# Routing the last token tile from values ahead of its layer norm, in a two-layer hybrid encoder step

## The reference, cut to what matters

```python
x = layernorm(DN_ALPHA * x + merged @ lp['w_out'], lp['ln1_g'], lp['ln1_b'])
moe_out = hier_moe(x, ...)
ple_term = jax.nn.sigmoid(x @ lp['w_ple_gate']) * (ple @ lp['w_ple'])
x = layernorm(DN_ALPHA * x + moe_out + ple_term, lp['ln2_g'], lp['ln2_b'])

def layernorm(x, g, b):            # mu, var over the row
    return (xf - mu) * lax.rsqrt(var + EPS) * g + b

# hier_moe: group logits x @ w_rg (4), expert logits x @ w_re (4 groups x 8)
g_top, g_idx = lax.top_k(softmax(x @ w_rg), 1)
e_top, e_idx = lax.top_k(softmax(e_logits of group g_idx), 2)
# each token goes to its two experts; h = silu(xb @ w1) * (xb @ w3); h @ w2; weighted sum
```

## Time and profile before

| | |
|---|---|
| time, median of 3 (lowest, highest) | 1543.61 us (1542.16, 1543.89) |
| profiled execution, its span | 1542.58 us, 1540.7 us |
| PE busy, weight loads | 1287.2 us (84%), 714.5 us (46%) |
| DVE, ACT, POOL busy | 400.0 (26%), 264.9 (17%), 56.3 us (4%) |
| memory traffic | 490.87 MB, mean 319 GB/s |
| mean granted clock | 0.928 |
| chain that ended last, by engine | PE 56%, DMA 33%, SP's queue 6%, DVE 3% |

### The profile page before, as it was taken

One profiled execution on the slowest core, in us unless ns is written; L12 is line 12 of the kernel. 1 busy time (PEld: TensorE's weight loads), 2 busy tenths in 40 slices (PEclk: granted clock), 3 DMA queues, 4 the chain that ended last, 5 costly groups with the idle time before them and its releaser, 6 DMA issues.

```text
span 1540.7 us, 20136 instructions
## 1 busy us (share of the span) xinstructions
PE 1287.2 (84%) x8464; PEld 714.5 (46%) x8465; DVE 400.0 (26%) x1021; ACT 264.9 (17%) x692; POOL 56.3 (4%) x98
## 2 busy tenths in 40 slices
PE   7999999999976766756699999999998766767655
PEld 4766887544431322322276678766353322313311
DVE  4142633532101101101133446245221101011003
ACT  2342422020100000000044434212110000000001
POOL 1300000000000000000022010000000000000000
PEclk9999999999988978888899999999999979879868
DMA  9503435989999999999972043578999999999994
GB/s 330 162 1 110 171 117 179 416 338 426 426 427 426 427 427 427 426 427 426 409 235 83 19 151 112 178 259 351 414 427 426 426 427 426 427 427 425 427 425 180
DMA packets 100047, 490.87 MB, mean 319 GB/s; under 512 B 9552, under 2 KB 15600, under 8 KB 52464
## 3 DMA queue, kind: packets, MB, share of 16 engines
q1 hardware_dynamic: 94912, 476.46, 75.8%
q0 software_dynamic: 5040, 13.03, 2.8%
HBM read 486.56 MB, written 2.89 MB: 318 GB/s over the span
## 4 chain that ended last, share of the span: by engine, by line
PE 56%; DMA 33%; SPq 6%; DVE 3%; issue 1%; ACT 0%; POOL 0%; DVEq 0%
PE bank L971 55%; DMA arena<-in_w_e_gate 12%; DMA arena<-in_w_e_up 9%; SPq L768 4%; DMA ring<-in_w_e_down 4%; DMA ring<-in_w_e_up 4%; SPq L834 2%; DMA ring<-in_w_e_gate 2%; DMA arena<-in_w_e_down 2%; PE bank L1021 2%; DMA ring<-in_w_in 1%; DVE arena L2062 0%; DVE arena L1950 0%; DVE x_sb L1959 0%; ACT xT L1570 0%
## 5 line engine op out<-in xcount | busy, mean ns | idle before, releaser
L971 PE MATMUL bank<-arena 128*32 128x512 f32 (+12 forms) x2696 | 496.9, 542 | 122.4 <-DMA arena<-in_w_e_gate 34.3
L971 PE MATMUL bank<-ring,arena 128*32 128x512 f32 (+4 forms) x1376 | 345.1, 645 | 2.7 <-ACT arena L1899 2.7
L971 PEld LDWEIGHTS bank<-arena 128*32 128x32 f32 (+4 forms) x2696 | 186.5, 138 | 335.6 <-issue 322.1
L971 PE MATMUL bank<-ring,xT 128*32 128x128 f32 (+5 forms) x1536 | 238.0, 364 | 1.4 <-ACT xT L1570 1.1
L971 PE MATMUL bank<-xT,ring 128*128 128x288 f32 x768 | 191.8, 407 | 0.0
L971 PEld LDWEIGHTS bank<-ring,xT 128*32 128x32 f32 (+1 forms) x1536 | 121.9, 137 | 101.1 <-issue 90.9
L971 PEld LDWEIGHTS bank<-xT,ring 128*128 128x128 f32 x768 | 143.7, 190 | 37.9
L971 PE MATMUL bank<-cst,arena 128*32 128x512 f32 x144 | 90.2, 785 | 57.2 <-DMA arena<-in_w_e_up 24.8
L971 PEld LDWEIGHTS bank<-ring,arena 128*32 128x32 f32 (+1 forms) x1376 | 87.4, 129 | 45.8 <-issue 36.6
L971 PE MATMUL bank<-arena,x_sb 128*128 128x128 f32 (+1 forms) x768 | 99.7, 282 | 1.4 <-DVE arena L2282 0.8
L971 PEld LDWEIGHTS bank<-arena,x_sb 128*128 128x128 f32 (+1 forms) x768 | 90.5, 190 | 20.1 <-issue 13.3
(11 more groups left out here) (225 smaller groups left out, 845.7 us busy)
## 6 DMA issues: line engine op xcount, KB each, us to landing
arena<-in_w_e_gate SPq DMA_DIRECT2D x68, 1024.0 KB, 26.0
arena<-in_w_e_up SPq DMA_DIRECT2D x62, 1024.0 KB, 26.5
arena<-in_w_e_down SPq DMA_DIRECT2D x58, 1024.0 KB, 26.3
ring<-in_w_e_up SPq DMA_DIRECT2D x48, 1024.0 KB, 26.6
ring<-in_w_e_gate SPq DMA_DIRECT2D x44, 1024.0 KB, 26.5
ring<-in_w_e_down SPq DMA_DIRECT2D x42, 1024.0 KB, 26.9
ring<-in_w_in SPq DMA_DIRECT2D x32, 1024.0 KB, 9.4
lb<-in_w_e_gate SPq DMA_DIRECT2D x14, 1024.0 KB, 25.9
```

Of the source, the lines that this page charges most:

```text
L971: return pe.matmul(out, lhsT, rhs, start=first, stop=last, skip_group_check=True)
```

## The change

Tile 1 is routed from its mixed values, ahead of the layer norm. With m the mean and r the inverse deviation of a row, the logits are

    ((x - m) * r * g + b) @ wr  =  r * (x @ (g * wr)  -  m * (g @ wr))  +  b @ wr

- POOL loads g and b of the first norm as columns (`norm_cols`, 16 numbers per partition) from a new input laid out on the host (`ln1_cols`). DVE multiplies the router's weights by g (`wr_scaled`).
- PE transposes the mixed tile (`turn_raw`), each half when DVE has written it (`x_mixed`), around `half_mix(1, 1)`. ACT copies both halves into xT.
- `router_sums` makes g @ wr and b @ wr, one row of 72 numbers, ACT moves it out of PSUM with the first half negated, `spread_sums` spreads it over 128 partitions, ACT moves it again.
- `router(1)` takes the raw transposes and `wr_scaled`; DVE corrects the logits in two operations, and the 14 routing operations follow.
- The norm's first pass runs ahead of the routing on DVE. The second pass (`shift_half`) runs in halves: one between the routing and `place_tile(1)`, one behind it. `ln_out` of tile 1 is signalled then.
- The transposes of the normalized tile (`turn_mixed(1)`), needed by its ple products, move behind "G" of quad 0, and PE waits for their copies ahead of `plain(0, 1)`.

```diff
@@ -214,7 +214,7 @@
             (("rt", 2), 7), (("t1", 0, 0), 0), (("t1", 0, 1), 1), (("wo", 0, 1), 6), (("rt", 0), 3),
-            (("rk", 2), 4), (("rk", 0), 5), (("wo", 1, 1), 2), (("t1", 1, 0), 0), (("t1", 1, 1), 1), (("rt", 1), 3),
+            (("rk", 2), 4), (("rk", 0), 5), (("raw", 0), 0), (("wo", 1, 1), 2), (("sw",), 7), (("raw", 1), 1), (("sb",), 7), (("rt", 1), 3),
             (("pl", 0, 2), 2), (("pg", 0, 2), 5), (("rk", 1), 4), (("XT0", 0), 6), (("XT0", 1), 7), (("cnt",), 3)]
@@ -237,7 +237,8 @@
     combine = [(job, b) for job, b in zip(COMBINE_JOBS, (7, 0, 1, 2, 3))]
-    j = [(("G",), 0)] + plain(0, 1, 2, 3) + ([(("ST0",), 4)] if g == 0 else []) + [(("U",), 1)] + plain(1, 0, 7, 0)
+    turned = [(("t1", 1, 0), 5), (("t1", 1, 1), 6)] if g == 0 else []
+    j = [(("G",), 0)] + turned + plain(0, 1, 2, 3) + ([(("ST0",), 4)] if g == 0 else []) + [(("U",), 1)] + plain(1, 0, 7, 0)
     if g:
...
@@ -531,6 +532,11 @@
         acc_s = carve(4544, D)
+        norm_cols = carve(0, 2, 8)
+        wr_scaled = carve(16, 8, 36)
+        wr_sums = carve(304, 72)
+        wr_sums_all = carve(376, 72)
+        raw_logits = carve(448, 36)
         scaled_s = carve(3072, 2 * P)
...
@@ -940,6 +949,7 @@
                 pool.dma_start(pT[:, :, SEQ:T], p_sample[layer]).then_inc(ple_in, 16)
+                pool.dma_start(norm_cols, ln1_cols[layer].rearrange("p (k c) -> p k c", k=2)).then_inc(norm_cols_in, 16)
                 job_read(pool, (layer, "bra", 3))
@@ -1289,17 +1299,34 @@
                         if c % 4 == 0:
-                            job_read(pe, (layer, "t1", t, c // 4))
-                        ins = mm(b[0:NT[t], 0:36], xT[:, c, T0[t]:T0[t] + NT[t]], wr[:, c, :], c == 0, c == 7)
+                            job_read(pe, (layer, "raw", c // 4) if t == 1 else (layer, "t1", t, c // 4))
+                        ins = mm(b[0:NT[t], 0:36], xT[:, c, now(t)], (wr_scaled if t == 1 else wr)[:, c, :], c == 0, c == 7)
                     done(ins)
+                def turn_raw(h):
+
+                    pe.wait_ge(x_mixed, 2 * layer + h + 1)
+                    transposes(layer, ("raw", h), [((c % 4) * P, P, x[0:P, 1, c * P:c * P + P]) for c in range(4 * h, 4 * h + 4)])
+
+                def router_sums():
+
+                    pe.wait_ge(norm_cols_in, 16 * (layer + 1))
+                    b = open_bank((layer, "sw"))
+                    for k in range(2):
+                        for c in range(8):
+                            ins = mm(b[0:1, 36 * k:36 * k + 36], norm_cols[:, k, c:c + 1], wr[:, c, :], k + c == 0, c == 7)
+                    done(ins)
+
+                def spread_sums():
+
+                    job_read(pe, (layer, "sw"))
+                    b = open_bank((layer, "sb"))
+                    done(mm(b[:, 0:72], ones[0:1, :], wr_sums[0:1, :], True, True))
+
                 def turn_mixed(t):
                     for h in range(2):
-                        if t == 1 and h == 0:
-                            pe.wait_ge(x_half, 2 * layer + 2)
-                        else:
-                            pe.wait_ge(ln_out, ln_place(2 * layer + 1, t))
+                        pe.wait_ge(ln_out, ln_place(2 * layer + 1, t))
                         transposes(layer, ("t1", t, h), [((c % 4) * P, P, x[0:NT[t], t, c * P:c * P + P]) for c in range(4 * h, 4 * h + 4)])
                 def plain_low(j, t):
@@ -1342,6 +1369,10 @@
                         for t in tiles:
+                            if t == 1 and h == 0:
+                                pe.wait_ge(x_half, 2 * layer + 2)
+                            elif t == 1:
+                                pe.wait_ge(ln_out, ln_place(2 * layer + 1, t))
                             for c in range(4):
@@ -1359,11 +1390,15 @@
                 rank(0)
+                turn_raw(0)
                 half_mix(1, 1)
+                router_sums()
+                turn_raw(1)
+                spread_sums()
+                pe.wait_ge(wr_scaled_out, layer + 1)
+                router(1)
                 pe.wait_ge(sel_early, layer + 1)
                 gather_first((2, 0))
-                turn_mixed(1)
-                router(1)
                 pe.wait_ge(ple_in, 32 * (layer + 1))
@@ -1489,6 +1524,9 @@
                     if g == 0:
+                        turn_mixed(1)
+                        for h in range(2):
+                            job_read(pe, (layer, "t1", 1, h))
                         plain(0, 1)
@@ -1834,9 +1872,25 @@
-                for t in MIX_ORDER:
+                def read_raw(h):
+
+                    key = (layer, "raw", h)
+                    job_done(act, key)
+                    emptied(act.copy(xT[:, 4 * h:4 * h + 4, now(1)], transposed(bank(key), 1)), key)
+
+                for t in (2, 0):
                     layer_norm(1 + 2 * layer, (t,))
-                    read_x("t1", layer, t, (0, 1) if t != 1 else (0,))
+                    read_x("t1", layer, t, (0, 1))
+                read_raw(0)
+                key = (layer, "sw")
+                job_done(act, key)
+                act.activation(wr_sums[0:1, 0:36], bank(key)[0:1, 0:36], ACT.Copy, scale=-1.0)
+                emptied(act.copy(wr_sums[0:1, 36:72], bank(key)[0:1, 36:72]), key)
+                read_raw(1)
+                layer_norm(1 + 2 * layer, (1,))
+                key = (layer, "sb")
+                job_done(act, key)
+                emptied(act.copy(wr_sums_all, bank(key)[:, 0:72]), key)
                 for t in MIX_ORDER:
@@ -1889,6 +1943,7 @@
                     if g == 0:
+                        read_x("t1", layer, 1, (0,))
                         plain_gate(0, 1)
@@ -2244,6 +2299,8 @@
                     job_read(dve, key)
+                    if t == 1:
+                        dve.sem_inc(x_mixed, 1)
                     step(half_stats(t, x[:, t, :], j))
@@ -2256,15 +2313,26 @@
                     job_done(dve, key)
+                    if t == 1:
+                        job_read(dve, (layer, "sb"))
+                        dve.wait_ge(ln_rstd, ln_place(1 + 2 * layer, t))
+                        step(dve.scalar_tensor_tensor(raw_logits, wr_sums_all[:, 0:36], mvs[:, 2:3], b[:, 0:36], ALU.mult, ALU.add))
+                        step(dve.scalar_tensor_tensor(raw_logits, raw_logits, ln_rs[:, 1:2], wr_sums_all[:, 36:72], ALU.mult, ALU.add))
+                        dve.sem_inc(bank_emptied[book.bank(key)], 1)
+                        b = raw_logits
                     step(dve.tensor_copy(lg[:, 0:4], b[0:n, 0:4]))
                     step(dve.max(r[:, 0:8], lg[:, 0:8]))
                     step(dve.max_index(ri[:, 8:16], r[:, 0:8], lg[:, 0:8]))
                     step(dve.tensor_copy(r[:, 16:17], ri[:, 8:9]))
                     step(dve.tensor_scalar(r[:, 48:52], iota[0:n, 0:4], r[:, 16:17], 2 * BIG, ALU.is_equal, ALU.mult))
-                    emptied(dve.scalar_tensor_tensor(lg[:, 8:40].rearrange("p (g e) -> p g e", g=GROUPS), bcast(r[:, 48:52], 2, PER_GROUP),
-                                                     BIG, b[0:n, 4:36].rearrange("p (g e) -> p g e", g=GROUPS),
-                                                     ALU.subtract, ALU.min), key)
-                    job_read(dve, key)
+                    ins = dve.scalar_tensor_tensor(lg[:, 8:40].rearrange("p (g e) -> p g e", g=GROUPS), bcast(r[:, 48:52], 2, PER_GROUP),
+                                                   BIG, b[0:n, 4:36].rearrange("p (g e) -> p g e", g=GROUPS),
+                                                   ALU.subtract, ALU.min)
+                    if t == 1:
+                        step(ins)
+                    else:
+                        emptied(ins, key)
+                        job_read(dve, key)
                     step(dve.max(r[:, 24:32], lg[:, 8:40]))
@@ -2289,6 +2357,8 @@
+                dve.wait_ge(norm_cols_in, 16 * (layer + 1))
+                dve.tensor_tensor(wr_scaled, wr, bcast(norm_cols[:, 0, :], 2, 36), ALU.mult).then_inc(wr_scaled_out, 1)
                 for t in (2, 0):
@@ -2303,10 +2373,24 @@
                 mixed(1, 1)
-                normalize(1 + 2 * layer, 1, x[:, 1, :], x_half)
-                read_x("t1", layer, xT, (1,))
+                at = ln_place(1 + 2 * layer, 1)
+                dve.bn_aggr(mvs[:, 2:4], ln_st).then_inc(ln_var, 1)
+                dve.wait_ge(ln_var, at)
+                job_done(dve, (layer, "raw", 1))
+                for h in range(2):
+                    half = x[:, 1, 512 * h:512 * h + 512]
+                    ins = dve.scalar_tensor_tensor(half, half, mvs[:, 2:3], lnw[:, 0, 512 * h:512 * h + 512], ALU.subtract, ALU.mult)
+                step(ins)
                 route_tile(1)
+
+                def shift_half(h):
+
+                    half = x[:, 1, 512 * h:512 * h + 512]
+                    return dve.scalar_tensor_tensor(half, half, ln_rs[:, 1:2], lnw[:, 1, 512 * h:512 * h + 512], ALU.mult, ALU.add)
+
+                shift_half(0).then_inc(x_half, 1)
```

(3 more changed lines are left out.)

8 lines of the change are left out of this document (6 added, 2 removed).

## The result

The changed kernel takes 1552.41 us (median of 8 runs, 1549.63 to 1558.61), the kernel before in the same runs 1543.46 (1542.01 to 1548.1). The ratio is 1.0056, 95% interval 1.0045 to 1.0067: slower by about 0.56%, by the medians 8.95 us, outside the range given. The profiled execution took 1552.71, its span is 1550.9, the mean granted clock 0.932.

The account below looks back on a forecast made before the run. The expert weight stream bounds the kernel, PE's work the start of G. Per layer +1.2 on G less 0.4 for the seam gives +0.8, for two layers +1.6: 1543.61 + 1.6 = 1545.2 us, range 1542.6 to 1548.8.

Parts of the forecast that it names:

- What bounds the stretch: Routing ahead of G of quad 0: PE's own work, almost without gaps, sets G's start, not the small vector operations.
- Rival A: Routing: the vector chain decides, so G begins 2.3 us a layer earlier and the time is 1538.9; chance 0.06.
- only change places: PE ahead of `rank(1)`: router product (1.88 us), gathers (4.25) and ple products (2.4) are reordered, adding nothing to the sum.
- The sum at full clock: PE's products put ahead of `rank(1)` less those taken off: G starts 1.2 us later per layer, ends +0.2 and +2.6.
- (a): PE ahead of `rank(1)`: the four transposes of `turn_raw(0)` add 0.5 us.
- (b): PE ahead of `rank(1)`: the 16 products of `router_sums` (32 rows in fp32) add 1.4 us, from 0.7 to 2.2.
- rival C: `router_sums` costs the count row's rate and the hand-off is long: +5.2 us in all, 1548.8; chance 0.13.
- (c): PE ahead of `rank(1)`: `turn_raw(1)` within the wait for ACT's reads, then `spread_sums`: 1.05 us, range 0.7 to 1.6.
- the 1.75 taken off: PE ahead of `rank(1)`: tile 1's transposes with their wait (1.37 us) and the rank product's wait (0.38) go.
- The seam: SP's queue: the later norm-slot piece lets the half pieces find a running stream, gaining 0.4 us a layer, between 0 and 0.9.
- `turn_mixed(1)` behind G: PE runs 2.0 us later behind G; queue backlog hides it, thinnest at the issue at 393.50 with 2.8 us in hand.
- rival B: Quad 1: the queue runs dry as the issue at 393.50 outlasts its cover, +3.6 us in all, 1547.2; chance 0.12.

Follow-up runs that it names:

- `after_b`: The changed kernel, unedited, profiled a second time to see where its granted clock falls; 1552.64 us, ratio 1.0059 to the kernel before.
- `before_thin`: The kernel before with 16 unused thin products (one weight column) put ahead of the router product of tile 1; 1546.69 us, ratio 1.002.
- `thin_ahead`: The kernel before with 48 unused thin products between the half mix and the gathers of tiles 2 and 0; 1553.25 us, ratio 1.0058.
- `before`: The kernel before the change, unedited, in its first profile; the profiled execution took 1542.58 us, with a span of 1540.70.
- `before_b`: The kernel before the change, unedited, profiled again; 1543.64 us, ratio 0.9995.
- `after`: The changed kernel, unedited, in its first profile; median 1552.41 us, ratio 1.0056 to the kernel before, profiled execution 1552.71.
- `shift_early`: The changed kernel with both halves of the norm's second pass ahead of `place_tile(1)` on DVE; 1550.45 us, ratio 1.0043 to the kernel before.
- `between_no_turn`: The changed kernel with gathers of tiles 2 and 0 ahead of spreading and router, and without `turn_mixed(1)` and its copies; 1551.96 us, ratio 1.0056 to the kernel before.
- `all3`: The changed kernel with sums around the layer's first mix, tile 2's ple products behind G, norm's second pass ahead of `place_tile(1)`; 1552.97 us, 1.0057 to the kernel before.

## Why the prediction was wrong

*What bounds the stretch: right.* PE has no gap from the half mix to `rank(1)`, which waits for nothing in all six layers of the changed kernel. Rival A, the vector chain, fell: in `after_b` `route_out` came 12.2 us behind the anchor instead of 14.6 and 3.2 us ahead of `rank(1)`, and G didn't start earlier. `before_thin` and `thin_ahead` move the issue by what they insert (0.84 for 0.89, 3.22 for 3.21).

*The step that failed: that the moved products cost nothing.* The prediction read 1.00 in the windows of the kernel before, which was right there, and went on from it to "TensorE's clock is not the cause" and to gathers and ple products that "only change places". Every term of its sum is at full clock, and no rival had another clock. In one of two layers the clock fell to 0.50 for 6.5 to 10.5 us. The gathers then took 7.23 us for 4.41 and the ple products 4.26 for 2.32 start to start; G comes 3.1 to 4.8 us later than in a layer without a fall, and the layer is 3.7 to 5.3 longer. That alone is more than the 3.6 us between the forecast and the range's upper end, and the border adds 1.6 at 0.50. Of the 8.9 us between the spans of `before` and `after_b`, 6.6 are such stretches. What the change costs at full clock, 2.2 us in layer 0 and 1.1 in layer 1, is twice the 1.6 forecast but inside the range. What in the order makes the clock fall stays open.

*The sum at full clock: 0.77 a layer instead of 1.2.* (a) 0.47 for 0.5. (b) 1.14 for 1.4; rival C with its 2.2 fell. (c) raw transposes, spreading and wait: 306.67 - 305.72 = 0.95 for 1.05; the hand-off was quicker, ACT read in 0.19 and 0.16. With the 1.75 taken off as worked out that makes 0.81, and G measured 0.77.

*The seam: wrong, small.* The norm-slot piece went out at 316.98 in `after_b`, without a fall, against 318.6 foreseen, and saved the stream nothing clear. In layer 0 the loss by +30 grew by 0.7 (8.84 in `after_b`, 8.15 in `before_b`) for a G 0.78 later, in layer 1 by 1.4 (9.33 in `after`, 7.95 in `before`) for 0.77. So it lies between a gain of 0.1 and a cost of 0.6, where a gain of 0.4 was taken. `shift_early`, with the piece earlier, had 8.89 in layer 1, which points at a cost.

*`turn_mixed(1)` behind G: right in size, wrong in cover.* `plain(0, 1)` starts 1.93 us behind G's end (2.0 foreseen). But the thinnest place is not 393.50. At 338.58, which the prediction showed and didn't time, a landing time of 8.6 us (8.7 in `before_b`) was not enough to give 2.1 away: the stream lost while the piece still landed in 6.6, so the 4.7 of a nearly empty queue isn't the point from which it costs. Between +30 and +114 the changed kernel without a fall loses 1.3 us in layer 0 and 0.5 in layer 1, the kernel before 0.1 to 0.3; `between_no_turn` takes the product away and most of the loss with it. So a loss of the kind of rival B came, 55 us earlier than placed (338.58 against 393.50) and smaller than its 3.6. The 4.4 us for a megabyte that the prediction took from the Trainium skill, page "DMA: Bandwidth & Descriptors", section "Anatomy of one DMA", is given there for DMAs that GpSimd issues; these pieces are issued by SP, and the sum didn't use it.

*What adds up.* From the spans of `before` and `after`: ahead of the first anchor -0.6; layer 0 +7.6, of it 5.3 the fall; the border to layer 1 +1.6, the clock; layer 1 +1.0; the end +0.6: 10.2 us. For `after_b`: -0.9, +2.3, +1.6, +6.1 (of it 5.0 the fall), -0.2 = 8.9. The border was not in the prediction at all. The kernel before has no fall there in two profiles and the changed kernel one in each of three; whether the change makes it more frequent wasn't tested.

## What to carry to other kernels

Where PE bounds a stage, count its work before the latency of small chains, and after a reordering look at the granted clock of each moved product in both layers and in several executions: a product that "only changes places" may cost nearly double. When a length varies between executions at a place that no edit touches, look at the granted clock there before anything else. Cover behind a stage is to be timed at every issue that the shifted work releases, the first one too, and a landing time above that of an empty queue didn't keep the stream whole here. Work moved out of the bound stage to behind it isn't free when the stage behind runs level with the stream (`all3`: G 2.3 us earlier, the stream 1.4 further behind by +114).
